# Value and gate projections of a three-mixer transformer kernel: ten blocks of 256 moving columns become five pairs with 512 moving columns

## The reference

```python
proj = h @ w_in                      # layer 0, "A": mLSTM, 8 heads, v of 128 per head, gates o_pre
v = proj[..., 1024:2048]; o_pre = proj[..., 2048:3072]
hs = sigmoid(o_pre) * normed(hs);    h = h + hs @ w_out

kv = rmsnorm(h, kv_norm_g) @ w_kv    # layer 1, "B": causal banded attention, 16 heads of 64
v_sh = kv[..., 1024:2048]

proj = h @ w_in_2                    # layer 2, "C": two branches
# branch a: differential attention, 4 heads, v_a = columns 1024:1536
# branch b: neighbourhood attention on an 8 x 64 grid, 8 heads, v_b = columns 2560:3072
merged = g_a * (y_a @ w_branch_a) + g_b * (y_b @ w_branch_b)
```

## Time and profile before

| | us |
|---|---|
| three runs | 1990.94, 1991.59 (median), 1992.21 |
| profiled execution, its own time | 1989.94 |
| its span, first to last instruction | 1988.2 |
| PE busy in it | 1969.0, 9948 matmuls |
| DVE, ACT busy | 1032.1, 715.7 |
| granted TensorE clock, mean | 1.000 |

### The profile page before, as it was taken

One profiled execution on the slowest core, in us unless ns is written; L12 is line 12 of the kernel. 1 busy time (PEld: TensorE's weight loads), 2 busy tenths in 40 slices (PEclk: granted clock), 3 DMA queues, 4 the chain that ended last, 5 costly groups with the idle time before them and its releaser, 6 DMA issues.

```text
span 1988.2 us, 25477 instructions
## 1 busy us (share of the span) xinstructions
PE 1969.0 (99%) x9948; PEld 1605.5 (81%) x9948; DVE 1032.1 (52%) x1454; ACT 715.7 (36%) x1063; POOL 18.8 (1%) x57
## 2 busy tenths in 40 slices
PE   9999999999999999999999999999999999999998
PEld 7988888888888777778888888766778998888887
DVE  6354665435465445575534556765445575533544
ACT  5442432212243444443212233444433462223232
POOL 0100000000000000000000000000000000000000
PEclk9999999999999999999999999999999999999999
DMA  4321333343233221233233224122323323233322
GB/s 156 95 66 52 117 85 85 95 116 85 82 93 128 100 80 55 86 84 101 84 106 106 77 85 141 64 64 63 103 74 100 112 65 105 81 104 90 102 71 82
DMA packets 299984, 180.79 MB, mean 91 GB/s; under 512 B 19180, under 2 KB 295765, under 8 KB 299901
## 3 DMA queue, kind: packets, MB, share of 16 engines
q1 hardware_dynamic: 288959, 178.90, 30.6%
q10 hardware_dynamic: 10941, 0.75, 0.4%
HBM read 175.80 MB, written 2.75 MB: 90 GB/s over the span
## 4 chain that ended last, share of the span: by engine, by line
PE 91%; DVE 4%; ACT 2%; SPq 1%; issue 1%; DMA 0%; DVEq 0%; ACTq 0%
PE psum L1727 28%; PE psum L1729 27%; PE psum L1728 27%; DVE wl L1106 1%; PE psum L1987 1%; PE psum L1939 1%; SPq L479 1%; PE psum L1948 1%; PE psum L1910 1%; PE psum L1962 1%; PE psum L2027 1%; PE psum L1998 1%; ACT wh L621 1%; PE psum L1877 1%; PE psum L2006 1%
## 5 line engine op out<-in xcount | busy, mean ns | idle before, releaser
L1106 DVE TENSOR_TENSOR wl<-stage,wh 128x2048 fp32r<-128x2048 f32 (+2 forms) x170 | 353.0, 2076 | 124.2 <-ACT wh L621 120.7
L621 ACT CAST wh<-stage 128x2048 fp32r<-128x2048 f32 (+2 forms) x164 | 283.3, 1728 | 218.7 <-PE psum L1729 210.0
L1727 PE MATMUL psum<-xl,wh 128*128 128x512 f32 (+1 forms) x768 | 304.8, 397 | 0.5 <-DVE wl L1670 0.5
L1727 PE MATMUL psum<-x2l,wh 128*128 128x512 f32 x768 | 302.8, 394 | 1.0 <-DVE wl L1106 0.6
L1729 PE MATMUL psum<-x2h,wh 128*128 128x512 f32 x768 | 299.1, 389 | 0.0
L1728 PE MATMUL psum<-x2h,wl 128*128 128x512 f32 x768 | 299.0, 389 | 0.0
L1729 PE MATMUL psum<-xh,wh 128*128 128x512 f32 (+1 forms) x768 | 293.1, 382 | 0.0
L1728 PE MATMUL psum<-xh,wl 128*128 128x512 f32 (+1 forms) x768 | 292.6, 381 | 0.0
L1727 PE MATMUL psum<-hidl,wh 128*128 128x512 f32 x528 | 205.8, 390 | 2.6 <-DVE wl L1106 2.6
L1728 PE MATMUL psum<-hidh,wl 128*128 128x512 f32 x528 | 205.5, 389 | 0.0
L1729 PE MATMUL psum<-hidh,wh 128*128 128x512 f32 x528 | 205.4, 389 | 0.0
(11 more groups left out here) (345 smaller groups left out, 2611.2 us busy)
## 6 DMA issues: line engine op xcount, KB each, us to landing
stage<-in_ffn_w_gate_dram SPq DMA_DIRECT2D x44, 512.0 KB, 4.0
stage<-in_ffn_w_up_dram SPq DMA_DIRECT2D x44, 512.0 KB, 5.2
stage<-in_w_in_dram SPq DMA_DIRECT2D x40, 512.0 KB, 4.0
stage<-in_ffn_w_down_dram SPq DMA_DIRECT2D x32, 384.0 KB, 3.6
stage<-in_a_w_in_dram SPq DMA_DIRECT2D x22, 512.0 KB, 4.6
stage<-in_w_gate_dram SPq DMA_DIRECT2D x22, 512.0 KB, 4.0
stage<-in_w_up_dram SPq DMA_DIRECT2D x22, 512.0 KB, 5.2
stage<-in_ffn_w_down_dram SPq DMA_DIRECT2D x32, 320.0 KB, 3.5
```

What stands on the lines that cost most here:

```text
L621: nc.scalar.copy(wh[:, par, 0:n], stage[:, par, 0:n]).then_inc(w_hi, 1)
L1106: vec.tensor_tensor(wl[:, par, 0:n], stage[:, par, 0:n], wh[:, par, 0:n].bitcast(F32), ALU.subtract).then_inc(w_lo, 1)
L1727: mm(out, a_hi, b_lo, start=start, stop=False)
```

## The change

- The values of head pairs 1 to 3 of A and their gates, the values of B's columns 0 to 511 and those of C's branch b become kind "wide": two blocks each (`A_w1`, `A_w2`, `A_w3`, `B_w0`, `C_wb`). Block i of a pair holds K tiles 4i to 4i+3 of 512 weight columns. In A these are 256 columns of v and 256 of o_pre.
- A wide pair uses all four banks 0 to 3, one for each token tile, and accumulates over both blocks. Its first unit waits as before for the block two before it; its ninth unit waits for the block just before it (`block_out >= b`).
- The eviction comes in halves of two token tiles, when the second block has done its units 7 and 15 (`evicted`, `wide_out`, semaphore `wide_done`). In A each half takes two instructions, in B and C one. DVE now evicts by the list `out` and no longer by `ended`.
- The order of blocks changes: A v1 o1 q1 k1 o2 v2 v3 o3 becomes w1 q1 k1 w2 w3; B v0 k1 q1 v1 k2 q2 ... becomes w0 k1 q1 k2 q2 ...; C ... kb0 vb0 qb1 kb1 vb1 becomes kb0 wb qb1 kb1. `B_RATE` and `C_RATE` change with it; the sums stay.
- `cvn` goes. `C_wb` is evicted into `cva`, after the last PV of branch a (`pv_done`). `place_values` runs once, with 32 DMAs of 16 partitions x 512 numbers, when both halves are evicted, and all PV matmuls of branch b wait for all 32.

```diff
-    for name in ("q0", "k0", "v0", "o0", "v1", "o1", "q1", "k1", "o2", "v2", "v3", "o3"):
-        add(f"A_{name}", {"v": "tokens", "o": "gate"}.get(name[0], "copy"), 1)
+    for name in ("q0", "k0", "v0", "o0", "w1", "q1", "k1", "w2", "w3"):
+        add(f"A_{name}", {"v": "tokens", "o": "gate", "w": "wide"}.get(name[0], "copy"), 2 if name[0] == "w" else 1)
...
+def evicted(stage, i, u):
+
+    if stage.kind != "wide":
+        return [i] if u == stage.units - 1 else []
+    return [u // 8] if i == 1 and u in (7, 15) else []
...
+            self.out.append([stage.b0 + first_half for stage, i, u in mine
+                             for first_half in evicted(stage, i, u)])
...
-B_RATE = [8] * 6 + [6] * 12 + [5] * 14 + [9] * 2
+B_RATE = [9] * 6 + [10, 6] + [5] * 24 + [9] * 2
...
-C_RATE = [6] * 24 + [7] * 8 + [4] * 2
+C_RATE = [6] * 16 + [7] * 8 + [6] * 8 + [4] * 2
...
+                if s.kind == "wide":
+                    r = DT // 2 * P * i
+                    if name[0] == "A":
+                        w, c = a_w_in[0], [n + 256 * int(name[3]) for n in (1024, 2048)]
+                    else:
+                        w, c = (w_kv, (D, D + 256)) if name[0] == "B" else (w_in[0], (2560, 2816))
+                    return [cols(w[r:r + DT // 2 * P, :], n, 256) for n in c], (DT // 2, 256)
...
                     load_one(s, s.name, i)
-                    if s.b0 + i - 4 in (st["C_vb0"].b0, st["C_vb1"].b0):
-                        place_values(s.b0 + i - 4)
-
-            def place_values(b):
-
-                c = 256 * int(blocks[b].name[4])
-                sp.wait_ge(block_out, b + 1)
+                    if s.b0 + i - 4 == st["C_wb"].b0:
+                        place_values()
+
+            def place_values():
+
+                sp.wait_ge(block_out, st["C_wb"].b0 + 2)
                 for r in range(NA_ROWS):
                     for k in range(NCB):
                         p = 64 * (r % 2) + 16 * k
-                        sp.dma_start(cvb[16 * r:16 * r + 16, k, c:c + 256], cvn[p:p + 16, r // 2, :]).then_inc(v_in, 16)
+                        sp.dma_start(cvb[16 * r:16 * r + 16, k, :], cva[p:p + 16, r // 2, :]).then_inc(v_in, 16)
...
+            def wide_out(s, i):
+
+                bank = 2 * ((s.b0 + i) % 2)
+                if i:
+                    dve.wait_ge(mm_done, s.b0 + 2)
+                else:
+                    dve.wait_ge(wide_done, 1 + ("A_w1", "A_w2", "A_w3", "B_w0", "C_wb").index(s.name))
+                dve.wait_ge(rst_ready, 1 + "ABC".index(s.name[0]))
+                t, ps = slice(2 * i, 2 * i + 2), psum[:, bank:bank + 2, :]
+                if s.name == "C_wb":
+                    dve.wait_ge(pv_done, C_HEAD0 + DA_HEADS)
+                    vec.tensor_tensor(cva[:, t, :], ps, rst[:, t, 0:1].to_broadcast([P, 2, 512]), ALU.mult
+                                      ).then_inc(block_out, 1)
+                    return
+                if s.name == "B_w0":
+                    parts = ((bv[:, 0:4, t, :], ps),)
+                else:
+                    c = 2 * int(s.name[3])
+                    parts = ((av[:, c:c + 2, t, 0:P], ps[:, :, 0:256]), (og[:, c:c + 2, t, :], ps[:, :, 256:512]))
+                for dst, src in parts:
+                    src = src.rearrange("p t (c n) -> p t c n", n=P)
+                    last = vec.tensor_tensor(dst.rearrange("p c t n -> p t c n"), src,
+                                             rst[:, t, 0:1].unsqueeze(2).to_broadcast(src.shape), ALU.mult)
+                last.then_inc(block_out, 1)
...
+                wide = s.kind == "wide"
                 if u == 0:
                     pe.wait_ge(w_lo, b + 1)
+                if u == 0 and not (wide and i):
                     pe.wait_ge(block_out, b - 1)
+                if u == 8 and wide and i == 0:
+                    pe.wait_ge(block_out, b)
...
+                if wide:
+                    t, kk = divmod(u, 4)
+                    k, token = 4 * i + kk, slice(t * P, (t + 1) * P)
+                    last = three(psum[:, (2 * (s.b0 % 2) + t) % 4, :], inh[:, k, token], inl[:, k, token],
+                                 whp[:, kk * 512:(kk + 1) * 512], wlp[:, kk * 512:(kk + 1) * 512], k == 0, k == DT - 1)
...
-                            pe.wait_ge(v_in, 512 * ((head - DA_HEADS) // 2 + 1))
+                            pe.wait_ge(v_in, 512)
```

More of the change, by code:

```diff
@@ L68, in plan @@
             for i in range(4):
-                add(f"B_v{i}", "tokens", 1)
+                if i != 1:
+                    add(f"B_{'v' if i else 'w'}{i}", "tokens" if i else "wide", 1 if i else 2)
                 if i < 3:
@@ L78, in plan @@
                 add(f"C_k{c}", "copy", 1)
-                add(f"C_v{c}", "tokens", 1)
+                if c[0] == "a":
+                    add(f"C_v{c}", "tokens", 1)
+                if c == "b0":
+                    add("C_wb", "wide", 2)
             add("C_ga", "copy", 4)
@@ L94, in plan @@
         s += DT if x.kind in ("residual", "down", "store") else 0
-        x.units = 16 if x.kind in ("tokens", "gate") else 2 * x.kt
+        x.units = 16 if x.kind in ("tokens", "gate", "wide") else 2 * x.kt
     for x, y in zip(order, order[1:] + [None]):
@@ L117, in __init__ @@
         assert sum(rate) == len(units), (sum(rate), len(units))
-        self.steps, self.ended, n = [], [], 0
+        self.steps, self.ended, self.out, n = [], [], [], 0
         for r in rate:
@@ L130, in part, with gates @@
         return mine[len(mine) * i // of:len(mine) * (i + 1) // of]
+    def gates(self, step, blocks):
+        both = [blocks[b] for b in self.out[step] if blocks[b].kind in ("gate", "wide") and b == blocks[b].b0 + blocks[b].blocks - 1]
+        return [int(s.name[3]) for s in both]
     def step_of(self, b):
@@ L185, in build @@
     a_names = [n for n in st if n[:2] == "A_" and n not in ("A_q0", "A_k0", "A_v0", "A_outB")]
-    c_names = [f"C_{q}{c}" for c in ("a1", "b0", "b1") for q in "qkv"] + ["C_ga"]
+    c_names = ["C_qa1", "C_ka1", "C_va1", "C_qb0", "C_kb0", "C_wb", "C_qb1", "C_kb1", "C_ga"]
     with ExitStack() as ctx:
@@ L837, in attention_a @@
                     if s >= 1:
-                        for b in a_stream.ended[s - 1]:
-                            if blocks[b].kind == "gate":
-                                gate_logarithm(b)
+                        for c in a_stream.gates(s - 1, blocks):
+                            gate_logarithm(c, st[f"A_{'w' if c else 'o'}{c}"].b0 + min(c, 1))
             def attention_b():
@@ L1147, in epilogue @@
                 both = rs[:, :].unsqueeze(1).to_broadcast([P, 2, S])
+                if s.kind == "wide":
+                    wide_out(s, b - s.b0)
+                    return
                 dve.wait_ge(mm_done, b + 1)
@@ L1163, in epilogue @@
                     c = int(name[4])
[L1164 to L1167, removed]
+                    vec.tensor_tensor(cva[:, :, c * 256:c * 256 + 256], ps.rearrange("p a (t n) -> p (a t) n", n=256),
                                       rst[:, :, 0:1].to_broadcast([P, TT, 256]), ALU.mult).then_inc(block_out, 1)
@@ L1439, in blocks_of_phase @@
                         if s >= 1:
-                            for b in a_stream.ended[s - 1]:
+                            for b in a_stream.out[s - 1]:
                                 epilogue_of(b)
@@ L1444, in blocks_of_phase @@
                         if s >= 2:
-                            for b in a_stream.ended[s - 2]:
-                                if blocks[b].kind == "gate":
-                                    gate_finish(b)
+                            for c in a_stream.gates(s - 2, blocks):
+                                gate_finish(c)
                     def probabilities(t):
@@ L1517, in attention_b @@
                     if 1 <= s <= len(b_stream.ended):
-                        for b in b_stream.ended[s - 1]:
+                        for b in b_stream.out[s - 1]:
                             epilogue_of(b)
@@ L1626, in attention_c @@
                     if 1 <= s <= len(c_stream.ended):
-                        for b in c_stream.ended[s - 1]:
+                        for b in c_stream.out[s - 1]:
                             epilogue_of(b)
```

27 lines of the change are left out of this document (16 added, 11 removed).

## The result

| | before | after |
|---|---|---|
| median of the runs, us | 1991.26 (1990.27 to 1992.21, 4 runs) | 2002.82 (2002.55 to 2003.48, 4 runs) |
| profiled execution, its own time | 1989.94 | 2003.48 |
| its span | 1988.2 | 2001.8 |
| PE matmuls | 9948 | 9468 |

The ratio is 1.0058 with a 95% interval of 1.0046 to 1.0070. The forecast was 2001 us, slower; the measured 2002.8 lies in its range. The profiled execution had been put at 1999.5 and took 2003.5, 4.0 us more.

The account below looks back on a forecast made before the run. PE's own program was taken as the bound. Terms -4.6 + 0.1 + 0.7 + 11.4 + 2.0 = +9.6 us put the profiled execution at 1999.5 and the median at 2001 us; range 1995 to 2004.5.

Parts of the forecast that it names:

- The placement: C step 21, PV of head 4: PE waits for 32 DMAs issued only from step 19; +11.4 us.
- the four rivals: In-time placement, 1987.8 (0.07); clock holds or quicker issue, 1996–1999 (0.16); longer hole, 2010–2020 (0.06); 4 us hole, 1992 (0.05).
- The clock: After PE's hole in C the granted clock is down for a time; +2.0 us, ends 0 and 3.9.
- The matmul form: 480 long matmuls replace 96 short ones in each of ten blocks; -4.6 us: 3.0 in A, 0.7 B, 0.9 C.
- evictions and banks: Wide pairs wait sooner for evicted banks, tightest in C step 18; +0.1 us, ends 0 and 1.
- My wrong reading of the earlier trace: Span start: 128-column matmuls read as 0.26 then 0.13 us each, bounding slow time after idleness to 7.7 us.
- B's rates: B steps 8 to 17 get five units, not six; steps 11 and 15 wait 0.35 us each, +0.7 us.
- the sentence that the loads stay at the same places and nothing waits for them longer: Weight loads stay two 512 KB DMAs per block, issued at the same places, with no longer waits; no cost.
- the 1.65 us: Added to the forecast sum: the profiled execution before lay this far below the runs' median, 1991.59 us.

Follow-up runs that it names:

- e1: Changed kernel with the values placed in two batches of 16 DMAs, the first once the first half is evicted; 1994.88 us, ratio 1.0017.
- e3: Changed kernel with the values sent through a DRAM scratch, 12 DMAs instead of 32, both halves' stores before the loads; 1990.41 us, ratio 0.9998.
- e9: Changed kernel with DRAM placement, other B rates, C's first bias tiles loaded later, plus nine dummy matmuls before the last sum of squares; 1984.97 us, ratio 0.9964.
- e5: Changed kernel with values through DRAM, each half stored and loaded once evicted, and other unit counts in B's steps 7 to 25; 1986.65 us, ratio 0.9973.
- e6: Changed kernel with wide pairs in A alone, B and C as in the kernel before, rates and order included; 1987.02 us, ratio 0.9977.
- e10: The changed kernel itself run once more, with no further edit; 2003.03 us.

## Why the prediction was right

**The placement (forecast 11.4 us, measured 11.8).** Every link came out: issues from 1382.99, 32 of them in 20.17 us, landing 1.9 us later, nothing gives it back. e1 and e3 show that it is the issue chain and its late start. Of the four rivals none took place.

**The clock (forecast 2.0, measured 1.6 to 2.9).** Right in kind and within its ends.

**The matmul form (forecast -4.6).** A gave 3.0 us, as worked out. This window of the changed kernel is the step with A's first scores, which took 6.28 us before:

```profile
65.91:72.06 6.15, 6.15 (x35) 4.63 (x34) 1.29 (x2) 1.91 (x1) 0.00 (x0) 1.00 0.16 15
```

Four of its seven units are long now, and it is 0.13 us shorter, 0.03 a unit.

In C, steps 13 to 15 took 0.43 us less, and step 15 fell from 6.00 to 5.84, the 0.17 of the forecast. Step 18 lost 0.15, where the forecast had 0.1 for evictions and banks. Over all of C, what is left of its 14.5 us after the wait (11.8), the clock (1.6) and the start (1.6) is a gain of 0.6; the forecast had 0.8 with the banks. My wrong reading of the earlier trace rows did not touch these terms; it bounded only how long the clock stays down.

**B's rates (forecast +0.7, measured about +1.6).** Steps 11 and 15 lost as said, but more: 0.5 and 0.75 us beyond the unit that was taken out, where the forecast had 0.35 each. Step 10, which had been counted as safe, lost 0.4. With the 0.7 gained by the long matmuls, B came out 0.9 us longer: 0.3 from its first to its last score and 0.6 ahead of the first score, where the third unit now stands.

**What was missing.** Three things that the working did not have come to 3.7 us: C's fourth weight block (1.6), the last transposes at half clock (1.7) and A's later beginning (0.4; with the same A it was between -0.3 and +0.5 in other kernels). B's rates (0.9), the wait (0.4) and C's gain (0.2) add 1.5. The clock in C cost 0.4 less than put and the tail behind the last matmul was 0.9 shorter. Together that is 3.9: the span grew by 13.5 us where the sum had 9.6. The tail belongs to the slow transposes, as e9 showed, so these cost 0.8 together. The weakest step of the working was the sentence that the loads stay at the same places and nothing waits for them longer. It looked at counts and places of the loads, but not at the slack of SP's queue ahead of C, where the fourth block had been in time by a little.

The medians miss by less, 2002.8 against 2001: the forecast put 1.65 us on its sum since the profiled execution of before lay that far under the median, and the profiled one of the changed kernel lay 0.7 above its own. That is luck in part. The profiled execution of before had a mean granted clock of 1.000, with which that kernel's runs were the fastest on average, so the 1.65 us stood in for falls of the clock that the working did not name.

## What to carry to other kernels

Two halves of a block that end together also hand over together: ask what each consumer waited for in the narrow form, and whether it can start with the first half. Where a chain of many small DMAs stands behind a late event, count the issues first, and only then the bytes. Here two stores and eight loads through DRAM behind the second eviction took the place of 32 DMAs and left a wait of 1.8 us; with the first half's four loads ahead of it, none was left. A program that gets shorter on the busiest engine moves towards every fixed chain beside it, so for each queue ask how much slack it has at the next stage boundary.

With the placement and B's rates mended, the changed kernel takes 0.9973 of the time before (e5), and with C's first loads and the end mended too 0.9964 (interval 0.9950 to 0.9977), where it had cost 0.6%. The last two mends do not need the wide blocks, and part of B's does not either. The kernel before was not run with them, so how much of the 0.4% is due to the change itself is not shown; wide pairs in A alone (e6) gave 0.9977.

## What the runs showed of the hardware

- An issue of a DMA on SP took 0.63 us from start to start for 16-partition pieces within SBUF, with 1 KB and with 2 KB rows alike (20.16 and 20.17 us for 32). In e3 the four stores to DRAM took 0.32 to 0.43 us each to issue and the eight loads from it 0.30 to 0.50.
- Among the first 32 bias tile loads of C exactly one issue was longer in each of the twelve profiles: 1.7 us before, 3.3 us in the changed kernel, at a median of 0.6. It changed between executions of one kernel as well (3.3 us in the changed kernel, 2.9 in e10, which is the same kernel).
- The granted clock fell during the 11.8 us hole, 4.8 us after the modelled end of the last score matmul at 1393.0 in one execution and 4.1 in another (e10). It was full again 3.3 and 6.0 us after PE restarted. In e1, whose wait was 4.4 us, it fell 3.8 us after the scores' end, 0.7 us before PE restarted, and was full again 2.8 us after.
- A wait of 2.2 us near the end was followed by the lower clock in seven of eleven profiles (the last 32 transposes 5.36 us in the changed kernel) and not in the others (3.69 us). In the changed kernel this moved the last transpose by 1.7 us and the end of the span by 0.8.
- One float32 matmul of 128 columns leaves two records and costs 0.226 us, as much as an fp32r matmul with 512 moving columns (0.227 us).
